# Taking the first product before the division at eight norms, and leaving out empty slots in a scatter

## The reference

```
# first block, layer i: six modulation vectors, two norms before and two behind
mod = silu(c) @ ada_w[i] + ada_b[i]        # (1024) @ (1024 x 6144), then split in six
h = rms_norm(x, g0) * (1 + sc_a) + sh_a
x = x + g_a * rms_norm(mixer(h), g1)       # first product of the mixer: h @ w_in
h = rms_norm(x, g2) * (1 + sc_f) + sh_f
x = x + g_f * rms_norm(square(relu(h @ ffn_w1[i])) @ ffn_w2[i], g3)
# second block, experts: rows of a token are gathered, go through its 8 experts,
# and are added back with weights
routed = zeros.at[slot_tok].add(expert(h[slot_tok]) * slot_w)
```

## Time and profile before

| | |
|---|---|
| median of 3 runs | 3758.86 us (3758.86 to 3766.8) |
| the profiled execution | 3765.87 us |
| its span, first to last instruction | 3764.2 us |
| PE busy | 3329.9 us, 88% |
| DVE busy | 1402.9 us, 37% |
| ACT busy | 504.7 us, 13% |
| POOL busy | 425.3 us, 11% |
| moved by DMA | 870.05 MB, 231 GB/s over the span |
| mean granted clock of PE | 0.953 |

### The profile page before, as it was taken

How to read it: one execution, slowest core, us unless ns; L and a number is a source line. 1 busy time by engine, 2 the same in 40 slices (tenths; PEclk the granted TensorE clock), 3 DMA queues, 4 the chain that set the end, 5 groups by cost and what they waited for, 6 DMA issues and landing times.

```text
span 3764.2 us, 40279 instructions
## 1 busy us (share of the span) xinstructions
PE 3329.9 (88%) x14228; PEld 2238.3 (59%) x14228; DVE 1402.9 (37%) x3085; ACT 504.7 (13%) x1021; POOL 425.3 (11%) x478
## 2 busy tenths in 40 slices
PE   3799897998999997889898897999894998999998
PEld 2678785887887886778664533434442676333333
DVE  7555615565013564574363322222213033111112
ACT  1210012000011002100031211111111021111111
POOL 0010102001000000000210311111112002000000
PEclk9899999999999999999999899999997999999999
DMA  7467532774434762366200479999994214998994
GB/s 291 179 240 283 225 135 89 291 274 160 157 111 180 290 268 90 135 245 234 100 34 12 164 255 349 384 376 376 363 368 145 101 59 175 382 388 367 414 369 188
DMA packets 136152, 870.05 MB, mean 231 GB/s; under 512 B 19248, under 2 KB 22448, under 8 KB 38448
## 3 DMA queue, kind: packets, MB, share of 16 engines
q1 hardware_dynamic: 94528, 675.32, 45.5%
q0 software_dynamic: 39984, 190.35, 15.5%
q10 hardware_dynamic: 1472, 2.18, 0.2%
HBM read 849.95 MB, written 36.18 MB: 235 GB/s over the span
## 4 chain that ended last, share of the span: by engine, by line
PE 71%; DMA 13%; DVE 8%; issue 4%; ACT 1%; POOL 1%; SPq 0%; DVEq 0%; POOLq 0%; ACTq 0%
PE ps L709 15%; PE ps L990 12%; PE ps L1230 10%; PE ps L973 9%; DMA ring<-stream_in 9%; PE ps L746 8%; PE ps L1252 6%; PE ps L1268 3%; DMA moe_out<-arena,slot_out 2%; DMA arena<-mod_stream_in 2%; PE ps L1199 2%; PE ps L735 1%; DVE arena L1733 1%; PE ps L1167 1%; DVE YS L1835 1%
## 5 line engine op out<-in xcount | busy, mean ns | idle before, releaser
L1230 PE MATMUL ps<-ring,arena 128*64 128x512 f32 (+2 forms) x2112 | 618.0, 630 | 79.2 <-DMA ring<-stream_in 79.2
L1733 DVE SCALAR_TENSOR_TENSOR arena<-arena,cond 128x512 f32<-128x512 f32 x630 | 447.6, 748 | 72.7 <-DMA arena<-mod_stream_in 62.7
L1230 PEld LDWEIGHTS ps<-ring,arena 128*64 128x64 f32 (+2 forms) x2112 | 224.7, 157 | 413.4 <-issue 411.6
L973 PE MATMUL ps<-H,ring 128*128 128x256 f32 x2048 | 453.9, 383 | 14.3 <-ACT H L1430 14.3
L990 PE MATMUL ps<-arena,ring 128*128 128x256 f32 x2048 | 445.9, 380 | 4.3 <-DVE arena L1995 4.3
L973 PEld LDWEIGHTS ps<-H,ring 128*128 128x128 f32 x2048 | 391.8, 193 | 68.2 <-issue 15.7
L990 PEld LDWEIGHTS ps<-arena,ring 128*128 128x128 f32 x2048 | 389.4, 191 | 56.6 <-issue 5.0
L1252 PE MATMUL ps<-ring,arena 128*64 128x512 f32 (+2 forms) x1056 | 314.4, 611 | 17.3 <-DMA ring<-stream_in 9.3
L1408 ACT ACTIVATE arena<-ps 128x512 f32<-128x512 f32 (+2 forms) x359 | 182.7, 509 | 861.3 <-PE ps L709 347.5
L2201 DVE TENSOR_TENSOR arena<-arena,ps 128x256 f32<-128x256 f32 x83 | 35.0, 421 | 653.3 <-ACT arena L1627 653.3
L746 PE MATMUL ps<-H,ring 128*128 128x256 f32 x1024 | 230.1, 389 | 24.5 <-ACT H L1430 14.3
(11 more groups left out here) (251 smaller groups left out, 3054.6 us busy)
## 6 DMA issues: line engine op xcount, KB each, us to landing
ring<-stream_in SPq DMA_DIRECT2D x618, 1024.0 KB, 9.2
arena<-mod_stream_in POOLq DMA_DIRECT2D x120, 1024.0 KB, 5.1
arena<-mod_stream_in SPq DMA_DIRECT2D x12, 1024.0 KB, 7.3
YS<-mod_stream_in SPq DMA_DIRECT2D x12, 1024.0 KB, 4.9
moe_out<-zeros POOLq DMA_DIRECT2D x10, 256.0 KB, 3.0
moe_in<-YS POOLq DMA_DIRECT2D x1, 2048.0 KB, 7.6
moe_out<-arena POOLq DMA_DIRECT2D x1, 2048.0 KB, 9.3
YS<-moe_out POOLq DMA_DIRECT2D x1, 2048.0 KB, 18.9
```

Source lines behind the costliest of these rows:

```text
L973: m = mm(out[:, i * T:(i + 1) * T], w[:, c * 256 + i * P:c * 256 + i * P + P], h_lat[c], start=(c == 0), stop=(c == DC - 1))
L1230: m = mm(out[at, :], e_xt[:, k % 2, 4 * part + c, at], w[:, c * TC:(c + 1) * TC], start=(part == c == 0), stop=(part == 1 and c == 3))
L1733: ins = stt(acc, w, x, acc, MUL, ADD)
```

## The change

**At a norm.** A product does not need its input divided: the deviation is one number for each token, which is a column of the output. `pre_norm` now has ACT write X * gain into H (256 columns), and the shift as a 257th column; PE multiplies these in `first_pair`, DVE divides the result by the deviation and adds the 257th column's result (`first_evicted`). PE's instructions alternate between the products of the pair's first half and those that sum the squares; the second half of the pair follows. Then DVE overwrites H with the divided input and ACT adds the shift, for all later pairs. ACT squares six chunks and DVE two, and DVE now does all eight additions to X, alternating with the scalings; POOL does none. The gains of the next layer are made before the reciprocal in `post_norm`.

**At the start.** Four modulation blocks of layer 0 instead of six; the other two move into layer 0's FFN, one to a turn, so a turn there has five blocks (`UP_WORK`). Of the four, PE does the second and the fourth (`by_products`: 32 products of 128 x 128 with one column each), DVE the others. The condition vectors have a transfer of their own, first in ACT's queue; SP issues all eight halves and eight ring pieces without waits. The sines of layer 0 move behind the latents' roots.

**Peeling.** The first turn of each FFN's loop is written out on PE, ACT and DVE (on ACT it was so in layer 0 only).

**The scatter.** `FAR` grows from 2 * TC to 4 * TC, past the end of the buffer, and the scatter gets a bound, so empty slots are left out. Rounds of one expert use the gather's indices; rounds of two have their own, no longer clipped.

```diff
-            order["mod", 0] = Phase([6, 5] * 3, 0)
+            order["mod", 0] = Phase([6, 0, 1, 2, 3] * 2, 0)
+UP_WORK = [[[(0, 0), (0, 1)], [(1, 0)], [(1, 1)], [(2, 0)], [(2, 1), (3, 0)], [(3, 1)], [(4, 0)], [(4, 1)]]]
+UP_WORK += [[[(j // 2, j % 2)] for j in range(8)] for _ in range(1, DEPTH)]
-FAR = 2 * TC
+FAR = 4 * TC
...
+                def by_products(i):
+                    outs = [bank(PLAN["mod", 0], 5 * (i // 2) + 1 + q) for q in range(4)]
+                    for half in range(2):
+                        weights, loaded, n = mod_piece_at(("start", 0), i, half, 0)
+                        pe.wait_ge(loaded, n)
+                        for q in range(4):
+                            for c in range(4):
+                                m = mm(outs[q][0][:, 0:1], weights[:, c, q * P:(q + 1) * P], cond[:, 4 * half + c, 0:1],
+                                       start=(half == c == 0), stop=(half == 1 and c == 3))
...
+            def first_pair(s, ph):
+                for c in range(DC):
+                    pe.wait_ge(h_raw, 9 * s + c + 2)
+                    m = mm(out[:, 0:T + 1], w[:, c, 0:P], raw_input(c), start=(c == 0), stop=(c == DC - 1))
...
+                    if c < 6:
+                        pe.wait_ge(sq_act, 8 * s + c + 1)
+                    else:
+                        pe.wait_ge(sq_dve, 4 * s + c - 5)
+                    m = mm(norm[:, 0:T], ones_d, SQ[:, c, :], start=(c == 0), stop=(c == DC - 1))
+                m.then_inc(norm_full, 1)
+                for c in range(DC):
+                    m = mm(out1[:, 0:T + 1], w[:, c, P:2 * P], raw_input(c), start=(c == 0), stop=(c == DC - 1))
+                    m.then_inc(h_raw_taken if c < DC - 1 else full1, 1)
...
             def pre_norm(s):   # ACT
-                for k in (0, 1):
-                    act.wait_ge(*((x_ready, 4 * s + 2 * k - 2) if s else (x_loaded, 16)))
-                    fn(SQ[:, 2 * k:2 * k + 2, :], X[:, 2 * k:2 * k + 2, 0:T], ACT.Square).then_inc(sq_act, 1)
+                fn(H[:, :, T:T + 1], mod[:, l, shift0:shift0 + DC].rearrange("p (c o) -> p c o", o=1), ACT.Copy).then_inc(h_raw, 1)
+                for c in range(DC):
+                    act.wait_ge(*((x_added, 8 * (s - 1) + c + 1) if s else (x_loaded, 16)))
+                    fn(H[:, c, 0:T], X[:, c, 0:T], ACT.Copy, scale=gains[:, l, 2 * (s % 2), c:c + 1]).then_inc(h_raw, 1)
+                    if c < 6:
+                        fn(SQ[:, c, :], X[:, c, 0:T], ACT.Square).then_inc(sq_act, 1)
...
+            def first_evicted(s, b, i, out):   # DVE
+                v.tensor_copy(first_shift[:, i:i + 1], ps[:, b, T:T + 1])
+                link(tt(out, ps[:, b, 0:T], RSTD[:, 0:T], MUL))
+                return ts(out, out, first_shift[:, i:i + 1], None, ADD)
...
+                def first_hidden():   # DVE, in an FFN ahead of the first modulation piece
+                    r = pairs(f_r[:, 0, :])
+                    first_halves(2 * l + 1, ph, [r[:, i, :] for i in range(2)])
+                    wait_drained(dve, ph, 0)
+                    link(ts(r, r, 0.0, None, ALU.max))
+                    tt(f_h[:, 0:2, :], r, r, MUL).then_inc(hidden_ready, 1)
...
-                        pool.indirect_dma_start(ff, bass.IndirectOffsetOnAxis(slot_out[:, at:at + 1], 0), e_y[:, k % 2, :], None,
-                                                compute_op=ADD).then_inc(scattered, 16)
+                        rows = slot_out if rounds[k].pair else slot_token
+                        pool.indirect_dma_start(ff[0:LANE_B + cols], bass.IndirectOffsetOnAxis(rows[:, at:at + 1], 0), e_y[:, k % 2, :], None,
+                                                bounds_check=LANE_B + cols - 1, oob_is_err=False, compute_op=ADD).then_inc(scattered, 16)
```

More of the change, by code:

```diff
@@ L163, in mod_plan @@
         n_turns = 1 if key[0] in ("start", "mla") else 2
-        steps = [8 * (1 if job[0] == "mod" else 2) for job in jobs]
+        adds = [1 if job[0] == "mod" else 2 for job in jobs]
+        steps = [0 if key[0] == "start" and i in START_BY_PE else 8 * adds[i] for i in range(len(jobs))]
         first = {}
@@ L619, in mod_adds @@
             m = MOD_PLAN[key]
-            return turn * (sum(m["steps"]) // 8) + (m["step"] + sum(m["steps"][:i])) // 8
+            return turn * sum(m["adds"]) + (m["add"] + sum(m["adds"][:i]))
         def mod_conds(key, i):
@@ L789, in mla @@
                 ph = PLAN["mla_in", l]
-                for k in range(2):
-                    pair(ph, k, k, h_lat, waits=wait_h(2 * l))
+                first_pair(2 * l, ph)
+                pair(ph, 1, 1, h_lat, waits=wait_h(2 * l))
                 j = l // 3
@@ L861, in stick @@
                 ph = PLAN["sb_in", l]
-                for k in range(8):
-                    pair(ph, k, k, h_lat, waits=wait_h(2 * l))
+                first_pair(2 * l, ph)
+                for k in range(1, 8):
+                    pair(ph, k, k, h_lat, waits=wait_h(2 * l) if k == 1 else None)
                 for k in range(4):
@@ L1539, in body @@
                 def body(turn):
-                    for j in range(8):
-                        k = j + len(mod_conds(("up", l), 0)) * (j // UP_PER_PAIR[l])
-                        b = wait_filled(act, ph, k, turn)
+                    for j in range(1 if isinstance(turn, int) and turn == 0 else 0, 8):
+                        b = wait_filled(act, ph, up_fill(l, j), turn)
                         n = turn * 8 + (16 * l + j - 1)
@@ new lines, in first_mods @@
+                dve.wait_ge(cond_ready, 2)
+                for half in range(2):
+                    mod_piece(("start", 0), 0, half, 0)
+                dve.wait_ge(consts_loaded, 64)
+                rope_tables(0)
+                mod_block(PLAN["mod", 0], 0, ("start", 0), 0, 0)
+                for half in range(2):
+                    mod_piece(("start", 0), 2, half, 0)
+                added_products(1)
+                mod_block(PLAN["mod", 0], 5, ("start", 0), 2, 0)
+                added_products(3)
@@ L1877, in mla @@
                     mod_pair(0)
-                drain(ph, 0, m_qlat, pairs)
+                first_halves(2 * l, ph, [m_qlat[:, c, :] for c in range(2)])
                 drain(ph, 1, region(512, 2, T), pairs)
@@ L2372, in post_norm @@
             def post_norm(s):
[L2374 to L2377 removed]
+                pool.wait_ge(y_scaled, 8 * s + 1)
             def mod_loads(key):
```

257 lines of the change are left out of this document (156 added, 101 removed).

## The result

The changed kernel takes 3743.57 us (median of four runs, 3742.49 to 3745.52) against 3762.83 (3758.86 to 3768.19) for the kernel before in the same comparison: a ratio of 0.9942, with a 95% interval of 0.9925 to 0.9959, so 15 to 28 us less. Forecast were 3678 us and a range of 3651 to 3708. The sign was right; the size was a quarter of what I said.

The account below looks back on a forecast made before the run. It took TensorE to bound the kernel nearly everywhere, with the transfer engines also full in the first expert layer. Scatter 52, norms 17 and start 12 sum to 81, taken from 3758.9 for 3678 us; range 3651 to 3708.

Parts of the forecast that it names:

- The scatter: First expert layer: leaving out empty slots' rows, 40% of each scatter, saves 52 us: middle 37, earlier rounds 5, tail 10.
- The period becomes 37.8: Middle of the first expert layer: three rounds fall from 40.9 to 37.8 us, still above PE's 35.2; 12 groups give 37.
- The tail's 10 us: End of the first expert layer: the last five scatters, each waiting for the one before, get 10 us shorter in all.
- Rival 1: First expert layer: a scatter pays only its bytes, so 27 us instead of 52, total 3703; chance 0.15.
- its limit: Rival 1's extreme: a skipped row costs like a written one, so the scatter gains nothing, 3730; chance 0.05.
- The start: Start of the kernel: DVE done with the gains at 48.4, 13.5 us earlier; the mixer loses 1.5, so 12 us less.
- rival 2: Start: weight loads of one-column products run at full pace, 7.0 us a block instead of 14.0, total 3668; chance 0.14.
- multiplies the second until 45.4: Start: PE multiplies one block from 16.3 to 30.3, transposes block 0, then multiplies its second block until 45.4.
- The norms: Dense layers: mixers of layers 1 to 3 gain 24.4; FFNs gain 1.2 and 4.0, lose 7.1, 1.8 and 3.3; sum 17.
- plus 1.5 as it starts at the lower clock: Norms: PE's interleaved products and sums need 7.0 us plus 1.5 for some 4 us at the lower clock, ending t0+10.2.
- rival 4: Norms: PE keeps the lower clock behind the interleaved sums, 3.6 us more a pair; slower than before, 3793; chance 0.03.
- rival 3: Norms pay nothing: waits for modulation blocks idle and slow PE, some 3 us more at each FFN; 3693; chance 0.14.

Follow-up runs that it names:

- spread_groups: Changed kernel with first expert layer's slots reordered, column j for place 32(j mod 4)+j/4 (half round 16(j mod 4)+j/4): 3695.8 us, ratio 0.9822 to the kernel before.
- warm: Changed kernel with nine unread products of constants on TensorE ahead of each interleaved pair of norms 1 to 7: ratio 0.9881 to the kernel before.
- up_plan: Changed kernel with the first modulation block of layer 0's FFN closed behind the second pair instead of the first: ratio 0.9913 to the kernel before.
- piece_early: Changed kernel with half of each FFN's first modulation block multiplied on DVE between the norm's squares and reciprocal: ratio 0.9875 to the kernel before.

## Why the prediction was right and wrong

**The scatter (forecast 52, measured 10): the step that failed.** It reads: "40% of it is 1.05 us", so "The period becomes 37.8". The first half held in the main: the queue's share fell by 6.1 points of 200 us, 12.2 us, 0.8 us for each of the 15 scatters. The second half put the mean over 16 engines in the place of the fullest. A piece of weights is there when its slowest sixteenth is, and twelve of the sixteen parts landed 7.3 to 12.1 us before that. By the map that fits the periods, the four fullest engines kept 21 to 22 of their 24 rows in three rounds, where the mean kept 14.8, and the period stayed at 41 us. The rows named the trap: a mean share of 101.9% with gathers that already skip, and I read it as "full" without asking of which engine. The tail's 10 us went the same way: 4.4 measured, since a lone scatter still took 6.3 us. With the rows in groups of four, evenly spread by the map, the sum comes out as I had written it: 37.7 for the period, 54 us in all. Rival 1 (only bytes count) would have been 3703, its limit 3730; neither mechanism is the right one, since bytes fell and nothing came of them, while with all rows skipped it gave 83 us more. Its 377 GB/s is the (62.73+12.59) MB of the earlier trace rows over 200 us; no run shows it as a limit, and spread_groups moved 391 GB/s in the same window.

**The start (forecast 12, measured about 6).** The one-column products were sized rightly, 13.8 us a block against 14.0, and rival 2 falls. I had read the earlier trace rows wrongly, though: its 64 columns are those that are multiplied, and each of its weight loads has 128, as here. The size was right because the start went at 0.213 us an instruction, the rate of that row at a granted clock of 0.50, and that it would I had not asked (the last section has the rows). The kernel before has 0.112 us for an instruction of 64 columns at a granted clock of 1.00, near the 0.11 of rival 2; no run shows that rate at the start, and it was in part luck that I took the slow row. The missing term is a queue: "multiplies the second until 45.4" left out that its four banks are those of the first, freed by copies that stand behind block 2's eight multiplications on the DVE. PE stood 7.4 us there. With the copies moved the gains come 14.3 us before the old start's and s0 11.2 before its mean, near the 12 of the forecast.

**The norms (forecast 17, by the stretches 5).** The mixers gave 19.1 of the 24.4, the FFNs lost 13.9 where I had 7. The reciprocal stands at t0+11.3 to 12.4 instead of 10.7: "plus 1.5 as it starts at the lower clock" was too small. The interleaved products take 8.7 to 9.8 us where 7.0 is needed at full clock (warm shows it, at a granted clock of 1.00), so 1.7 to 2.8. I had taken 0.333 us for an instruction of 256 columns at the lower clock by counting six in a window of 2 us at a granted clock of 0.50, which counts those that reach over its ends; by their starts it is 0.427 at 0.50, against 0.216 at 1.00. No run shows the 0.333, and rival 4's price for a slow pair, 32 x (0.333-0.22), was too low for the same reason. Warmed, the seven norms are 2.7 us shorter each. The idle behind the first pair in layers 1 and 2, 3.7 us, was in the plan (20.8 to 24.8 there, plus the lower clock, "perhaps slow, 26.1"), but it was set 0.7 for the slow clock where the row shows 2.1. Layer 1 lost another 1.7 to a drop of the granted clock further on, to 0.50 from 801.2 to 804.6 us, in the products of its second matrix; the kernel before has 1.00 in the same window, and why it falls is open. Layers 0 and 3 came out as forecast (+9.7 for +8.9, +3.2 for +3.3). The 257th column cost next to nothing: 3.63 us for the 16 instructions of half a pair, against a quarter of the 14.05 for 64, 3.51. Rival 4, a clock that stays low, did not come: at the first norm the granted clock is 0.51 from 200.4 to 203.8 us and 1.00 from 204.0 to 207.9; rival 3 was nearer than my own number: 5 us is close to nothing.

So 3743.6 is 66 us above the forecast: 42 from the scatter, some 6 from the start, 12 from the norms, and 4 because the kernel before took 3762.8 in this comparison and not the 3758.9 that I started from; 2 are left. The range failed because its upper end, rival 1, still let the scatter gain 27; the "limit" at 3730, given 0.05, was the honest end.

## What to carry over

A share of DMA time is a mean over 16 engines, while a transfer ends with its slowest part: here twelve of sixteen parts landed 7.3 to 12.1 us ahead of the last. Before pricing rows that are skipped, count them for what ends last, not in the mean. Here padded slots laid out so that every group of four neighbouring rows holds near and far places took the period from 40.6 to 37.7 us. Where an engine is handed work in another's gaps, follow each bank back to the instruction that frees it and to what stands ahead of that in its queue. TensorE idled some 4 us (median 4.3) ahead of the fine-grained exchanges here, and the lower clock afterwards (0.51 granted from 200.4 to 203.8 us, 0.50 from 466.7 to 470.0) cost another 2 to 3 us: idle products, or a piece of other work done early on the engine it waits for, bought 19 and 24 us.

## What the hardware showed that I had not expected

- Leaving out 40% of a scatter's rows changed neither the period (41.0 against 40.9 us) nor a lone scatter's time (6.3 us); as many left out alike in every group of four rows gave 37.7 and 4.6 to 4.9.
- Twelve of the sixteen parts of a piece of weights landed 7.3 to 12.1 us ahead of the last, and their lead did not speed up anything: the period stayed at 41.0 us.
- The 64 instructions of a block of one-column float32 products, each with a weight load of 128 columns, take 13.8 us, 0.213 from start to start. The row that I had compared them with has the same loads (first line), 0.214 apart at a granted clock of 0.50. Products of 64 columns elsewhere in the kernel before are 0.112 apart at a granted clock of 1.00 (second and third line). The loads fill 6.90 of the row's 7.06 us. So an instruction of 64 columns takes 0.214 us at 0.50 and 0.112 at 1.00; no run here shows how it goes with the columns of the load.

```profile
3139.60 6.90 PEld L709 LDWEIGHTS ps<-ring,H 128*128 128x128 f32 x32 [6.96 <-issue]
...
2098.11 1.06 PE L709 MATMUL ps<-arena,tab 128*128 128x64 f32 x8
...
2098.00:2099.00 1.00, 1.00 (x11) 1.00 (x11) 0.00 (x0) 0.00 (x0) 0.58 (x1) 1.00 0.96 373
```

- A granted clock of 1.00 at the very start is no measurement. The window of the changed kernel prints it, but the trace's first clock record is at 60.5 us, and the view prints 1.00 where it has none:

```profile
20.00:22.00 2.00, 2.00 (x11) 2.00 (x11) 1.83 (x6) 0.00 (x0) 0.00 (x0) 1.00 1.03 414
...
28.59 1.09 PE L747 MATMUL ps<-tab,stat 128*128 128x128 f32 x4
```

  The times of the products stand in its place. The four transposes (second line) take 1.09 us; four such take 1.11 in up_plan at a granted clock of 0.50 (222.3 to 223.3 us) and 0.66 in piece_early at 1.00 (658 to 661 us). Instructions of 256 and 257 columns are 0.427 us apart until 60.5 us, as from 467.4 to 469.9 us at a granted clock of 0.50, and 0.216 from there on, at a granted clock of 1.00. The one-column products are 0.213 us apart, as the earlier trace rows at 0.50. From these I take it that both blocks ran at the lower level; no clock record shows it. At 0.112 us each a block would take 7.2 us, an estimate; no run here shows that rate at the start.
